# Two more column groups of w_in in the first quarter of the k-blocks, and another deal of the w_ada chunks

## The reference

```python
mod = silu(c) @ w_ada + b_ada            # 12288 columns, in six parts
shift_a, scale_a, gate_a, shift_f, scale_f, gate_f = split(mod, 6)
h = rms_norm(x, g_attn_pre) * (1 + scale_a) + shift_a
proj = h @ w_in                          # 2048 x 5456
d_q, d_k, d_v, s_q, s_k, s_v, i_q, i_k, i_w = split(proj)
diff_out = differential_attention(rope(d_q), rope(d_k), d_v)   # 8 heads
dsa_out  = indexed_sparse_attention(rope(s_q), rope(s_k), s_v, rope(i_q), rope(i_k), i_w)
mixed = concat(diff_out, dsa_out) @ w_o
x = x + gate_a * rms_norm(mixed, g_attn_post)
```

## Time and profile before

| | |
|---|---|
| three timed runs | 2328.56, 2329.45, 2329.59 us |
| profiled execution | span 2329.2 us; no time of it stands beside the span |
| TensorE, VectorE, ScalarE busy | 97%, 61%, 46% of the span |
| w_in starts, its second quarter starts | 37.46 us, 83.90 us |
| w_in's quarter 3 ends, about | 182 us |
| the wait for ("d", 4) in w_o ends | 409.55 us |

### The profile page before, as it was taken

The page is one execution under the profiler, slowest core; times in us unless marked ns, Lnnn a source line. Parts: engine busy times, 40 slices in busy tenths (PEclk is TensorE's granted clock), DMA queues, the critical chain, the costliest instruction groups (busy, mean ns, idle before and its releaser), DMA issues.

```text
span 2329.2 us, 25922 instructions
## 1 busy us (share of the span) xinstructions
PE 2257.8 (97%) x10584; PEld 1844.7 (79%) x10584; DVE 1417.5 (61%) x1922; ACT 1073.0 (46%) x1489; POOL 0.7 (0%) x5
## 2 busy tenths in 40 slices
PE   6899898999999999999999999999999999999998
PEld 3677677878888888888887878888888888888887
DVE  6899987876764654554456545454545555554555
ACT  3435445544444444434445555555344444444443
POOL 0000000000000000000000000000000000000000
PEclk9999999999999999999999999999999999999999
DMA  9988676756875755555554544444555555555553
GB/s 394 404 324 338 247 289 263 286 201 235 299 263 197 251 201 186 194 195 185 196 184 149 211 159 154 158 154 163 199 193 186 194 185 190 189 186 194 187 192 144
DMA packets 79510, 507.69 MB, mean 218 GB/s; under 512 B 8352, under 2 KB 18848, under 8 KB 19744
## 3 DMA queue, kind: packets, MB, share of 16 engines
q1 hardware_dynamic: 79392, 506.05, 58.9%
HBM read 501.82 MB, written 4.19 MB: 217 GB/s over the span
## 4 chain that ended last, share of the span: by engine, by line
PE 87%; DVE 6%; DMA 3%; ACT 3%; issue 1%; SPq 0%; DVEq 0%; ACTq 0%
PE bank L655 27%; PE bank L657 27%; PE bank L656 27%; DMA raw<-in_chunks_dram 3%; DVE wlo L1832 2%; PE bank L698 1%; PE bank L790 1%; DVE raw L1822 1%; ACT whi L1182 1%; PE bank L706 1%; DVE raw L1817 1%; PE bank L619 0%; PE bank L813 0%; PE bank L793 0%; DVE P L1996 0%
## 5 line engine op out<-in xcount | busy, mean ns | idle before, releaser
L1832 DVE TENSOR_TENSOR wlo<-raw,whi 128x1024 fp32r<-128x1024 f32 (+2 forms) x746 | 896.5, 1204 | 804.0 <-ACT whi L1182 803.3
L1182 ACT ACTIVATE whi<-raw 128x1024 fp32r<-128x1024 f32 (+2 forms) x746 | 776.1, 1044 | 956.2 <-PE bank L657 906.8
L655 PE MATMUL bank<-whi,Ahi 128*128 128x512 f32 (+2 forms) x2304 | 908.6, 394 | 30.4 <-DVE wlo L1832 20.1
L657 PE MATMUL bank<-whi,Alo 128*128 128x512 f32 (+2 forms) x2304 | 894.4, 388 | 0.0
L656 PE MATMUL bank<-wlo,Ahi 128*128 128x512 f32 (+2 forms) x2304 | 894.1, 388 | 0.0
L655 PEld LDWEIGHTS bank<-whi,Ahi 128*128 128x128 f32 x2304 | 435.6, 189 | 131.9 <-DVE wlo L1832 31.2
L657 PEld LDWEIGHTS bank<-whi,Alo 128*128 128x128 f32 x2304 | 435.4, 189 | 89.7
L656 PEld LDWEIGHTS bank<-wlo,Ahi 128*128 128x128 f32 x2304 | 436.1, 189 | 83.0
L655 PE MATMUL bank<-whi,Fhi 128*128 128x512 f32 x352 | 137.6, 391 | 0.0
L657 PE MATMUL bank<-whi,Flo 128*128 128x512 f32 x352 | 137.0, 389 | 0.0
L656 PE MATMUL bank<-wlo,Fhi 128*128 128x512 f32 x352 | 137.0, 389 | 0.0
(11 more groups left out here) (305 smaller groups left out, 1386.2 us busy)
## 6 DMA issues: line engine op xcount, KB each, us to landing
raw<-in_chunks_dram SPq DMA_DIRECT2D x435, 1024.0 KB, 4.8
P<-in_chunks_dram SPq DMA_DIRECT2D x14, 1024.0 KB, 11.4
G<-in_chunks_dram SPq DMA_DIRECT2D x7, 1024.0 KB, 11.3
raw<-in_chunks_dram SPq DMA_DIRECT2D x8, 768.0 KB, 4.2
raw<-in_chunks_dram SPq DMA_DIRECT2D x8, 576.0 KB, 4.2
raw<-in_chunks_dram SPq DMA_DIRECT2D x4, 672.0 KB, 12.3
x<-in_x_turned_dram SPq DMA_DIRECT2D x2, 1024.0 KB, 12.9
x<-in_x_dram SPq DMA_DIRECT2D x4, 512.0 KB, 7.9
```

Of the source, the lines that this page charges most:

```text
L655: pe.matmul(o, a_hi, w_hi, start=beg and kk == 0, stop=False)
L657: ins = pe.matmul(o, a_lo, w_hi, start=False, stop=fin and kk == 1)
L1182: act.activation(m.whi[:, i % NHL, :, 0:n], m.raw_of(c)[:, 2 * h:2 * h + 2, 0:n], ACT.Copy).then_inc(m.s_hi, 1)
L1832: dve.tensor_tensor(m.wlo[:, i % NHL, :, 0:n], m.raw_of(c)[:, 2 * h:2 * h + 2, 0:n], m.whi[:, i % NHL, :, 0:n].bitcast(F32), ALU.subtract) ...
```

## The change

Groups 1 and 7 also run in quarter 0, behind group 2, and later only with quarters 1 to 3 (`left_of`). Their quarter-0 sums are copied out by ScalarE, and the sums of the three later quarters are added by VectorE (`add_part`) in place of ScalarE's copy. The twelve w_ada chunks behind quarter 0 (eleven before) are dealt 2, 1, 2, 1, 2, 2, 2 over its seven groups; the eight for the next quarter are used behind the first five. `first_scale` then stands after group 2 and `first_shift` after group 1 in quarter 0, and after group 9 and group 0 in quarters 1 and 2.

```diff
 W_IN_FIRST = (10, 8, 9, 0, 2)
+W_IN_EXTRA = (1, 7)
+W_IN_PARTS = (W_IN_FIRST + W_IN_EXTRA, W_IN_FIRST, W_IN_FIRST, W_IN_FIRST)
+SCALE_AFTER = ((0, 2), (1, 9), (2, 9))
+SHIFT_AFTER = ((0, 1), (1, 0), (2, 0))
 W_IN_ORDER = (4, 6, 1, 3, 5, 7)
-DEAL_PE = ((3, 3, 2, 2, 1), (2, 2, 1, 1, 1), (2, 2, 2, 0, 0), (0, 0, 0, 0, 0))
-DEAL_VECTOR = ((0, 0, 0, 0, 0), (0, 0, 0, 0, 0), (0, 0, 0, 1, 1), (1, 1, 1, 1, 2))
+DEAL_PE = ((2, 1, 2, 1, 2, 2, 2), (2, 1, 1, 2, 2), (2, 1, 1, 0, 0), (0, 0, 0, 0, 0))
+DEAL_VECTOR = ((0, 0, 0, 0, 0, 0, 0), (0, 0, 0, 0, 0), (0, 0, 0, 1, 1), (1, 1, 1, 1, 2))
+def left_of(cg):
+    return (4, 8, 12) if cg in W_IN_EXTRA else (0, 4, 8, 12)
@@ chunk_plan
-        for i, cg in enumerate(W_IN_FIRST):
+        for i, cg in enumerate(W_IN_PARTS[q]):
-        m = 4 * len(W_IN_ORDER)
+        m = sum(len(left_of(cg)) for cg in W_IN_ORDER)
     for cg in W_IN_ORDER:
-        for q in range(4):
-            lin("w_in", 4 * q, *win_cols(cg))
+        for k0 in left_of(cg):
+            lin("w_in", k0, *win_cols(cg))
-WIN_ITEMS = [(q, cg) for q in range(4) for cg in W_IN_FIRST]
+WIN_ITEMS = [(q, cg) for q in range(4) for cg in W_IN_PARTS[q]]
+WIN_LAST = len(WIN_ITEMS) - len(W_IN_FIRST)
@@ tensor_program (the other engines alike)
-    for q, cg in WIN_ITEMS[:3 * len(W_IN_FIRST)]:
+    for q, cg in WIN_ITEMS[:WIN_LAST]:
         first_part(q, cg)
-        if cg == W_IN_FIRST[3]:
+        if (q, cg) in SHIFT_AFTER:
             ada_columns(q + 1)
@@ scalar_program
     for cg in W_IN_ORDER:
         c0, n = win_cols(cg)
-        s = linear("w_in", c0, n, before=first_mix if cg == W_IN_ORDER[-1] else None)
+        s = linear("w_in", c0, n, ks=left_of(cg), before=first_mix if cg == W_IN_ORDER[-1] else None)
...
         for tb in range(2):
-            evacuate(s, tb, m.P1[:, tb, c0:c0 + n], ACT.Copy, n)
+            if cg not in W_IN_EXTRA:
+                evacuate(s, tb, m.P1[:, tb, c0:c0 + n], ACT.Copy, n)
@@ vector_program
+    def add_part(s, c0, n, cg):
+        for tb in range(2):
+            o = m.P1[:, tb, c0:c0 + n]
+            need.wait_ge(m.s_mm, k.unit)
+            released(part_at[cg, tb])
+            dve.tensor_tensor(o, o, m.out_bank(s, tb, n), ALU.add).then_inc(m.freed[2 * s + tb], 1)
...
     for cg in W_IN_ORDER:
-        s = linear("w_in", *win_cols(cg), before=first_mix if cg == W_IN_ORDER[-1] else None)
+        s = linear("w_in", *win_cols(cg), ks=left_of(cg), before=first_mix if cg == W_IN_ORDER[-1] else None)
+        if cg in W_IN_EXTRA:
+            add_part(s, *win_cols(cg), cg)
```

More of the change, by code:

```diff
@@ L933, in tensor_program @@
     jobs = lane_jobs(indexer, sparse, differential)
-    for q, cg in WIN_ITEMS[3 * len(W_IN_FIRST):]:
+    for q, cg in WIN_ITEMS[WIN_LAST:]:
         s = first_part(q, cg)
@@ L953, in tensor_program @@
     for cg in W_IN_ORDER:
-        s = linear("w_in", *win_cols(cg), m.A_op, shifted(0), before=first_mix if cg == W_IN_ORDER[-1] else None)
+        s = linear("w_in", *win_cols(cg), m.A_op, shifted(0), ks=left_of(cg),
+                   before=first_mix if cg == W_IN_ORDER[-1] else None)
         k.P_at[cg] = [(2 * s, k.at[s][0]), (2 * s + 1, k.at[s][1])]
@@ L1295, in scalar_program @@
     first_operand(0)
-    for q, cg in WIN_ITEMS[:3 * len(W_IN_FIRST)]:
+    for q, cg in WIN_ITEMS[:WIN_LAST]:
         first_part(q, cg)
-        if cg == W_IN_FIRST[2]:
+        if (q, cg) in SCALE_AFTER:
             gather(q + 1)
-        if cg == W_IN_FIRST[3]:
+        if (q, cg) in SHIFT_AFTER:
             first_operand(q + 1)
@@ L1989, in first_part @@
         s = linear("w_in", c0, n, ks=(4 * q,))
+        if q:
+            add_part(s, c0, n, cg)
         for tb in range(2):
[L1991 to L1997, removed]
+            part_at[cg, tb] = set_at(s)[tb]
         return s
```

## The result

The change makes the kernel slower: 2342.56 us median (2339.27 to 2343.37, four runs) against 2329.52 of before (2328.56 to 2330.29, four runs); ratio 1.0055, 95% interval 1.0043 to 1.0068, that is +13.0 us. Forecast were 2335.0 with a range to 2340.5. The direction was right, the loss more than twice as large, and the time lies outside the range. The profiled execution took 2343.37, the longest of the four, and its span is 2341.7. About 1.67 us lie between time and span in the runs of this kernel, and 1.3 in those of before that are on record, so some 0.4 us of the loss stand outside the span.

What follows compares the result with a forecast made beforehand. TensorE, busy 97% of 2329.2 us, was taken as the bound, so reordering only wins or loses its idle or slowly clocked time. -6.2 + 3.0 + 1.0 + 8.0 = +5.8 gave 2335.0 us, range 2324.5 to 2340.5.

Steps and rivals of the forecast that it cites:

- term C: End of w_in: group 7's add and one more w_ada chunk cost +1.0 us, bounds 0 and 3.8, VectorE's lead hiding most.
- term D: Wait for ("d", 4): two more steps run uncovered, with head 7's softmax; +8.0 us, bounds 2.9 and 9.5.
- Term A: First quarter: the second starts 5.2 us later with 11.4 us more work done; -6.2 us, bounds -8.5 and -3.
- The rival in which the first quarter gives nothing: Ring slots are freed late behind the tables, loads pause; first quarter only -2, total +10, 2339.2 us; chance 0.08.
- One side sum: Third quarter's tightest load: at about 358 GB/s, 2.93 us a chunk, it lands 8 us late; first-quarter term about +2.
- Term B: Top-k on VectorE: group 1's add and two w_ada halves lengthen TensorE's waits; +3.0 us, bounds 1.2 and 3.8.
- The first rival ("costs little"): Wait for ("d", 4): the two bare steps overlap existing waiting, cost 2.9; total +0.7, 2329.9 us; chance 0.29.
- the second ("faster"): First quarter wins its 6.2 us, other slack takes up the two steps; total -5.0, 2324.2 us; chance 0.17.
- From there to the end the same length: From w_o's column group 1 at k-block 8 to the end, the same length as before.

Runs made afterwards that it cites:

- only_1: Changed kernel with group 1 alone taken into the first quarter, group 7 whole, w_ada chunks dealt two to each of six groups; 2326.40 us, ratio to before 0.9986.
- only_7: Changed kernel with group 7 alone taken into the first quarter, group 1 whole, w_ada chunks dealt two to each of six groups; 2339.45 us, ratio to before 1.0036.
- experiment 7: Kernel before, with the wait for ("d", 4) one chunk earlier, so six bare steps with the jobs' lag untouched; 2332.98 us, ratio to before 1.0015.
- experiment 5: Changed kernel with the job of sparse pairs 2 and 3 starting two steps later, six bare steps kept; 2333.24 us, ratio to before 1.0012.

## Why the prediction was wrong

Most of its mechanism held, and its sum was too small: +5.8 against +12.5 between the spans. The step that failed most is term C, the end of w_in, where VectorE's lead was to hide most of the cost; next to it stand 2.3 us behind the wait for which there was no term, and in term D 2.2 us that were taken off and did not come off. The forecast also set a span equal to a time, though 1.3 us lie between them in before and 1.67 in the change. Term by term, in the profiled executions:

- **Term A, the first quarter: forecast -6.2, measured -6.5.** The second quarter starts at 90.25 (forecast 89.1: group 2 starts 0.5 later than forecast, and the products of `ada_columns`, 0.9 us at 82.71, stood in no item). Before the fourth quarter the 1.0 of the w_ada chunk has come back, where I had counted it as lost. The loads don't pause, and one gap over 3 us is left, 4.46 (forecast 4.4). The half clock that I priced at 1.5 behind it came: the chunk of group 2 takes 7.28 us at a mean clock of 0.77, which is 1.7 us.

```profile
67.77:75.05 7.28, 7.28 (x24) 5.56 (x24) 6.12 (x9) 2.61 (x4) 0.00 (x0) 0.77 1.01 428
```

  The first product behind the gap still takes 0.50, since the clock fell just behind it. What no longer comes is the gap of 3.84 at 46.23 with its slow clock. The rival in which the first quarter gives nothing falls. One side sum does not come out: with its 2.93 us a chunk from entry 12 (43.86) on, entry 43 would land at 134.7, 11 us late and not 8.
- **Term B, the top-k: forecast +3.0, measured +3.8.** It is the w_ada chunk: with `only_1` the add is there and the gaps are those of before. From 179.49 to the product behind the first gap it is 1.3 us longer, from there to that behind the second 1.3 again (9.99 for 8.65), each one w_ada half of 1.28. (The second gap itself grew by 1.6, but 0.3 of that is TensorE ending sooner, with 4.7 us at the lower clock behind the first gap instead of 5.2.) The last 1.1 come up to 309.07, with a gap of 0.72 there. I had the halves at 1.2, and half of the add in the gaps; it stands behind them, at 286.03. With `W_IN_SHARE` 22 the term falls to about 0.5, add and all. It ends at the upper bound that I gave.
- **Term C, the end of w_in: forecast +1.0, measured +3.4. This is the step that failed most.** I wrote that VectorE "has about 2 us of lead over TensorE here, which hides most", and looked at VectorE's work alone. What the runs showed: the load of w_o's second chunk waits for the slot of a w_ada chunk, so it is late, ScalarE stands for 5.72 us, and a finish of another job stands behind it; TensorE waits 2.28 at 373.46 for that and 4.83 instead of 3.22 at 383.55. That SP's order costs "nothing" I had decided from the first quarter. With `W_IN_SHARE` 22 the late load is gone and the term falls from 3.4 to about 0.5 (306.93 to 377.68, against 309.87 to 383.55 here). That run takes the second w_ada chunk off VectorE as well, so how much of the 3.4 is the load and how much the work on VectorE was not measured apart. A further gap, 1.69 at 322.27 for the sparse scores, is in every kernel with group 1 moved and not in before or `only_7`; it too stood in no item.
- **Term D, the wait for ("d", 4): forecast +8.0, measured +9.4.** The stretch itself came out as forecast: from the end of the last covered product (401.94) it is 17.8 us, forecast 17.8, with the sparse exponentials ahead of head 7's finish. From start to start it is 9.1 longer than before, forecast 9.2. What failed is the 2.2 of TensorE work that I took off again, as work that the covered stretches would lose. The four half chunks ahead of the wait did not get shorter:

```profile
383.55:401.55 18.00, 18.00 (x85) 14.97 (x85) 12.36 (x22) 7.86 (x25) 0.00 (x0) 0.84 0.64 238
```

  Before, they took 17.65 at a mean clock of 0.90, so clock alone makes 1.1 us of difference: it is at the lower level behind the gap of 4.83 until 389.2, and was so behind the gap of 3.22 until 387.1. The clock behind the wait, which I put at 1.0, is not in the 9.4 at all, since it falls behind 419.72: 5 us at a mean of 0.64, which is 1.8. The runs split the term: two more bare steps cost 3.2 with the old lag (experiment 7; I had 2.9 as the lower bound), and the rest goes with the lag of the two jobs. In the timed runs the lag is worth 9.3 (experiment 5), more than the term has left; where that comes from is told there. The first rival ("costs little") falls with it, and with the sum the second ("faster").
- **"From there to the end the same length": it is 2.3 longer.** 0.7 of this comes in w_o, where the 1.8 of slow clock behind the wait are in part taken back, and 1.3 right behind a gap of 2.87 that stands in every one of these kernels. I had no term for it, and the 1.3 may be chance.

The misses, 0.8 + 2.4 + 1.4 + 2.3 less 0.3 in A, give 6.6 of the 6.7. Each of B, C and D lay inside its own bounds, all near the upper one. The bounds summed reach -3 + 3.8 + 3.8 + 9.5 = +14.1, or 2343.3; the range stopped at 2340.5, as if they would not all go wrong together. They did. In C I counted an engine's own work and not what stood behind it in program order; in B and D the pieces were right in kind, and a price or a deduction was off.

## What to carry to other kernels

When work is taken out from under several jobs that share engines in program order, look first at the lag between the jobs, and only then at how much cover is left: here a lag of 14 steps instead of 16 cost 9.3 us, and two `yield`s gave them back, while two steps without cover cost 3.2. An extra chunk at a place has two prices, the time of the engine that uses it and the slot that it holds; the second showed here as an idle engine "waiting for a DMA" while the loads ran at half rate just before. And take the parts of a change by themselves, and then together: one of the two groups moved here wins 3.6 us, the other one costs 9.5, and the pair costs 13.0.

## What the runs showed of the hardware

The same gap, in the same code, is not followed by the same clock. At the border behind w_o every one of these kernels has a gap of 2.87 us, and the granted clock of the 10 us behind it is 0.83 in before, 0.69 in the changed kernel and 1.00 in `only_1`. The rows, in this order:

```profile
498.42:508.42 10.00, 10.00 (x45) 8.46 (x46) 6.94 (x11) 4.32 (x6) 0.00 (x0) 0.83 0.30 107
```

```profile
509.34:519.34 10.00, 10.00 (x39) 8.39 (x40) 6.36 (x10) 3.16 (x4) 0.00 (x0) 0.69 0.29 105
```

```profile
495.18:505.18 10.00, 10.00 (x52) 8.51 (x53) 7.39 (x12) 5.11 (x7) 0.00 (x0) 1.00 0.30 107
```

Since the clock has the two levels 1.2 and 2.4 GHz, a mean of 0.69 is about 6 of 10 us at the lower one, and one of 0.83 about 3. Between the ends lie 3.1 us for one gap, nearly as much as `only_1` wins. Over the fourteen kernels profiled here it is 1.00 in two, 0.83 to 0.85 in ten, and 0.69 or 0.70 in two. What decides which it will be stays open. It need not be the kernel: over the eleven timed runs of `only_1` the mean granted clock of a whole run lies between 0.990 and 0.993, with 2324.95 us at 0.993 and 2328.84 at 0.990. So a difference of one or two us between two profiled executions says little by itself. Of the 5.6 us by which the spans of before and `only_1` differ, 1.7 are this clock; the timed difference is 3.6.
